# A second layer's modulation vectors: from condition matmuls in a merge stage to row products on the vector engine

## What is computed

```python
def modulation(cond, w, b):
    m = jax.nn.silu(cond) @ w + b
    return jnp.split(m, 3, axis=-1)

for l in range(DEPTH):                                   # DEPTH = 2
    sh, sc, gt = modulation(c, ada_w[l], ada_b[l])       # ada_w[l]: 1024 x 3072
    shc, scc, gtc = modulation(c_ctx, ada_w[l], ada_b[l])
    h = rms_norm(x, norm_pre[l]) * (1.0 + sc[:, None]) + sh[:, None]
    hc = rms_norm(xc, norm_pre[l]) * (1.0 + scc) + shc
    ...
    x_new = x + gt[:, None] * rms_norm(out, norm_post[l])
```

## Time and profile before

| what | value |
|---|---|
| median of 3 runs | 2044.37 us (2043.87 to 2047.22) |
| the profiled execution, its own time | 2042.73 us |
| its span, first to last instruction | 2040.9 us |
| mean granted TensorE clock | 0.986 of full |
| TensorE matmul busy | 1960.0 us, 96% |
| VectorE busy | 1296.8 us, 64% |
| ScalarE busy | 978.1 us, 48% |
| GpSimd busy | 30.3 us, 1% |
| bytes moved | 351.84 MB, mean 172 GB/s |

### The profile page before, as it was taken

The page is one execution under the profiler, slowest core; times in us unless marked ns, Lnnn a source line. Parts: engine busy times, 40 slices in busy tenths (PEclk is TensorE's granted clock), DMA queues, the critical chain, the costliest instruction groups (busy, mean ns, idle before and its releaser), DMA issues.

```text
span 2040.9 us, 29528 instructions
## 1 busy us (share of the span) xinstructions
PE 1960.0 (96%) x12558; PEld 1702.9 (83%) x12558; DVE 1296.8 (64%) x1748; ACT 978.1 (48%) x1457; POOL 30.3 (1%) x23
## 2 busy tenths in 40 slices
PE   7799999999999999999989999999999999989998
PEld 3699999899888889999878887678888888768887
DVE  3877756878645778865565565755557555676555
ACT  1355445465334546534454445554445444565444
POOL 1300000000000000000000000000000000000000
PEclk8899999999999999999999999999999999999999
DMA  7544555434676533455445554355555555525554
GB/s 307 194 155 145 163 180 170 149 125 135 212 252 229 195 128 129 144 188 181 161 140 191 186 166 161 109 167 189 189 175 178 193 186 186 176 73 176 186 187 143
DMA packets 95410, 351.84 MB, mean 172 GB/s; under 512 B 10608, under 2 KB 10736, under 8 KB 94768
## 3 DMA queue, kind: packets, MB, share of 16 engines
q1 hardware_dynamic: 94032, 341.08, 50.6%
q0 software_dynamic: 960, 7.37, 0.9%
q10 hardware_dynamic: 288, 1.51, 0.2%
HBM read 348.87 MB, written 1.05 MB: 171 GB/s over the span
## 4 chain that ended last, share of the span: by engine, by line
PE 83%; DVE 11%; ACT 3%; DMA 2%; issue 1%; SPq 0%; DVEq 0%; ACTq 0%
PE PS L551 25%; PE PS L553 24%; PE PS L552 24%; DVE w_lo L1805 3%; DMA raw<-weights 2%; ACT w_hi L1293 1%; PE PS L629 1%; PE PS L723 1%; PE PS L954 1%; PE PS L742 1%; PE PS L917 1%; PE PS L1036 1%; PE PS L806 1%; PE PS L732 0%; PE PS L1047 0%
## 5 line engine op out<-in xcount | busy, mean ns | idle before, releaser
L1805 DVE TENSOR_TENSOR w_lo<-raw,w_hi 128x1024 fp32r<-128x1024 f32 x600 | 733.2, 1232 | 400.4 <-ACT w_hi L1293 399.0
L1293 ACT ACTIVATE w_hi<-raw 128x1024 fp32r<-128x1024 f32 x600 | 624.8, 1055 | 409.4 <-DMA raw<-weights 404.7
L551 PE MATMUL PS<-h_hi,w_hi 128*128 128x256 f32 x1568 | 455.3, 290 | 14.5 <-DVE h_lo L1823 5.4
L552 PE MATMUL PS<-h_lo,w_hi 128*128 128x256 f32 x1568 | 445.2, 284 | 0.0
L553 PE MATMUL PS<-h_hi,w_lo 128*128 128x256 f32 x1568 | 445.1, 284 | 0.0
L551 PE MATMUL PS<-w_hi,h_hi 128*128 128x512 f32 (+1 forms) x1024 | 389.2, 380 | 8.7 <-DVE h_lo L2171 6.5
L553 PE MATMUL PS<-w_hi,h_lo 128*128 128x512 f32 (+1 forms) x1024 | 380.7, 372 | 0.0
L552 PE MATMUL PS<-w_lo,h_hi 128*128 128x512 f32 (+1 forms) x1024 | 379.4, 370 | 0.0
L551 PEld LDWEIGHTS PS<-h_hi,w_hi 128*128 128x128 f32 x1568 | 302.1, 193 | 33.1 <-issue 18.9
L552 PEld LDWEIGHTS PS<-h_lo,w_hi 128*128 128x128 f32 x1568 | 302.4, 193 | 0.6 <-issue 0.5
L553 PEld LDWEIGHTS PS<-h_hi,w_lo 128*128 128x128 f32 x1568 | 302.2, 193 | 0.0
(11 more groups left out here) (256 smaller groups left out, 1855.0 us busy)
## 6 DMA issues: line engine op xcount, KB each, us to landing
raw<-weights SPq DMA_DIRECT2D x642, 512.0 KB, 3.4
x<-weights SPq DMA_DIRECT2D x6, 512.0 KB, 10.2
layer<-layer_in POOLq DMA_DIRECT2D x2, 1536.0 KB, 11.4
cx<-ctx_in POOLq DMA_DIRECT2D x1, 1024.0 KB, 8.5
x<-x_in POOLq DMA_DIRECT2D x1, 1024.0 KB, 12.5
out<-arena SPq DMA_DIRECT2D x4, 256.0 KB, 2.0
consts<-consts_in POOLq DMA_DIRECT2D x1, 928.0 KB, 9.2
arena<-filter_consts_in ACTq DMA_DIRECT2D x1, 896.0 KB, 8.3
```

Of the source, the lines that this page charges most:

```text
L551: pe.matmul(dst, hi, m_hi_, start=first, stop=False, **kw)
L552: pe.matmul(dst, hi, m_lo_, start=False, stop=False, **kw)
L1293: nc.scalar.activation(w_hi[:, r, :], raw[:, r, :], ACT.Copy).then_inc(w_hi_ready, 1)
L1805: V.tensor_tensor(w_lo[:, r, :], raw[:, r, :], f32(w_hi[:, r, :]), ALU.subtract).then_inc(w_lo_ready, 1)
```

## The change

Layer 1's modulation is no longer computed with matmuls. Its weights are packed transposed: a slot now holds 128 output features by 1024 inputs, so that a feature's row lies along a partition. Both condition rows are loaded in 128 copies (`cond_in`, 1 MB), once in each of passes 0 and 1, and ScalarE takes their silu in place. For each slot VectorE makes two products, one for each condition: a scalar_tensor_tensor that multiplies slot and condition row and puts the sum along the row into one column of `ada_sums`. There are 24 slots and so 48 products, 24 in pass 0 and 24 in pass 1, three behind each attention unit's splits. The slots are loaded by GpSimd's queue into two buffers. These, the condition rows and the products' outputs lie in the area of `g_hi` and `g_lo`, which is free from the merge of one pass (or, before pass 0, from the spectra) to the gating of the next; a wait ahead of the first gate's write keeps the order. `mod_vectors(1)` reads `ada_sums`. The merge of pass 1 becomes the same as in the other passes, and the ring carries 24 slots fewer. Layer 0's modulation stays.

```diff
+ADA_ENDS = [0, 12, ADA_SLOTS]
...
-    stretch("pass1", dram_pass[0], MERGE_AT)
-    stretch("pass1_merge", None, MERGE_SLOTS + ADA_SLOTS)
-    stretch("pass1_wo", dram_pass[0] + MERGE_AT + MERGE_SLOTS, 8)
+    stretch("pass1", dram_pass[0], PASS_SLOTS)
...
+        beside = nc.alloc_sbuf_tensor_at("beside", [P, 6, SLOT], F32, offset=g_at)
+        cond_rows, ada_w, ada_prod = (beside[:, 2 * j:2 * j + 2, :] for j in range(3))
...
+        ada_sums = sb("ada_sums", [P, 48])
...
             spectrum_bias(0)
+
+            def load_ada(n):
+                pool.dma_start(ada_w[:, n % 2, :], weights[dram_pass[1] - ADA_SLOTS + n]).then_inc(ada_w_loaded[n % 2], 16)
+
+            def modulation_rows(part_):
+
+                first, end = ADA_ENDS[part_], ADA_ENDS[part_ + 1]
+                pool.wait_ge(spec_pair, DEPTH)
+                pool.dma_start(cond_rows[:, :, :], cond_in).then_inc(cond_loaded, 16)
+                load_ada(first)
+                load_ada(first + 1)
+
+                for n in range(first + 2, end):
+                    pool.wait_ge(ada_sum, 2 * (n - 1))
+                    load_ada(n)
+
+            modulation_rows(0)
+            pool.wait_ge(w_used, start["pass1"])
+            modulation_rows(1)
...
-                        if p == 1:
-                            ada(c, b, 0, i)
-                            c += 1
...
-                        if p == 1:
-                            ada(c + 1, b, 1, i)
-                            c += 1
                         pair(c + 1, 2 * b + 1)
-                    if p == 1:
-                        ada_turn(ADA_TURNS + i, 7)
...
+            def cond_silu(part_):
+
+                act.wait_ge(cond_loaded, 16 * (part_ + 1))
+                nc.scalar.activation(cond_rows[:, :, :], cond_rows[:, :, :], ACT.Silu).then_inc(cond_rows_act, 1)
...
                 splits(c0 + 6)
+                if p < 2:
+                    cond_silu(p)
                 splits(c0 + part["v"])
...
+            def ada_row(i):
+
+                n, w = divmod(i, 2)
+                dve.wait_ge(ada_w_loaded[n % 2], 16 * (n // 2 + 1))
+                if i >= 2:
+                    dve.wait_ge(ada_sum, i - 1)
+                V.scalar_tensor_tensor(ada_prod[:, w, :], ada_w[:, n % 2, :], 1.0, cond_rows[:, w, :], ALU.mult, ALU.mult,
+                                       accum_out=ada_sums[:, i:i + 1]).then_inc(ada_sum, 1)
+
+            def ada_rows_behind(p, first, end):
+                if p < 2:
+                    dve.wait_ge(cond_rows_act, p + 1)
+                    for i in range(2 * ADA_ENDS[p] + first, 2 * ADA_ENDS[p] + end):
+                        ada_row(i)
...
+                    if p < 2 and (b, j) == (0, 0):
+                        dve.wait_ge(ada_sum, 2 * ADA_ENDS[p + 1])
                     link(V.tensor_copy(g_hi[:, s, :], gd))
...
                     splits(c0 + part["v"] + 2 + 2 * n)
+                    ada_rows_behind(p, 3 * n, 3 * n + 3)
...
-                        if p == 1:
-                            ada_piece(c + 1, ADA_TURNS + i, b, (6, 7))
...
+            for c in range(0, 3 * D, P):
+                slots.append(g["ada_w"][l][:, c:c + P].T)
```

More of the change, by code:

```diff
@@ L118, in build @@
     dram = dram_pass[1] + PASS_SLOTS
-    for p in (0, 2):
+    for p in range(3):
         start[f"pass{p}_merge"] = start[f"pass{p}"] + MERGE_AT
@@ L300, in build @@
         ada_used = sem("ada_used")
+        cond_loaded = sem("cond_loaded")
+        cond_rows_act = sem("cond_rows_act")
+        ada_w_loaded = [sem(f"ada_w_loaded{j}") for j in range(2)]
+        ada_prod_ready = sem("ada_prod_ready")
+        ada_sum = sem("ada_sum")
         raw_loaded = [sem(f"raw_loaded{r}") for r in range(RING)]
@@ L413, in build @@
         block = ctx.enter_context(nc.Block())
-        def is_ada(c):
-            n = c - start["pass1_merge"]
-            return 0 <= n < MERGE_SLOTS + ADA_SLOTS and n % 5 in (0, 2)
-        def splits_to(c):
-            return c + 1 - sum(is_ada(a) for a in range(start["pass1_merge"], min(c + 1, start["pass1_wo"])))
         def f32(ap):
@@ L631, in ada_half @@
                 return mm
-            def ada(c, m, half, i):
-                if half == 0 and m == 1:
-                    pe.wait_ge(ada_taken, ADA_TURNS + i)
-                if half == 0 and m == 2:
-                    pe.wait_ge(ada_rows_ready, 3 * ADA_TURNS + 1 + 3 * i)
-                r = c % RING
-                pe.wait_ge(raw_loaded[r], 16 * (c // RING + 1))
-                ada_half(raw[:, r, :], 6 + m % 2, half).then_inc(w_used, 1)
             def ada_turn(turn, bank):
@@ L845, in run_pass @@
                 pe.wait_ge(act_evac, act_pairs(p, 9))
-                each = 5 if p == 1 else 3
                 for i in range(4):
                     for b in range(3):
-                        c = start[f"pass{p}_merge"] + each * (3 * i + b)
-                        if p == 1:
-                            ada(c, b, 0, i)
-                            c += 1
+                        c = start[f"pass{p}_merge"] + 3 * (3 * i + b)
                         pe.wait_ge(merge_free, i * 3 + (15 * p + b + 1))
@@ L1479, in run_pass @@
                 gates("gc", 2)
-                each = 5 if p == 1 else 3
                 for i in range(4):
                     for b in range(3):
-                        c = start[f"pass{p}_merge"] + each * (3 * i + b)
-                        for j in range(-1, each - 1):
+                        c = start[f"pass{p}_merge"] + 3 * (3 * i + b)
+                        for j in range(-1, 2):
                             split(c + j + AHEAD)
                         act.wait_ge(merge_free, i * 3 + (15 * p + b + 1))
-                        act.wait_ge(w_used, c + each)
+                        act.wait_ge(w_used, c + 3)
                         nc.scalar.activation(sel[:, b, :], PS[:, 2 * b + 1, :], ACT.Sigmoid).then_inc(sel_ready, 1)
@@ L2113, in run_pass @@
                 V.memset(signal[:, 1:2], 0.0).then_inc(merge_free, 1)
-                each = 5 if p == 1 else 3
                 for i in range(4):
                     for b in range(3):
-                        c = start[f"pass{p}_merge"] + each * (3 * i + b)
-                        for j in range(-1, each - 1):
+                        c = start[f"pass{p}_merge"] + 3 * (3 * i + b)
+                        for j in range(-1, 2):
                             split(c + j + AHEAD)
-                            if p == 1 and j == 2:
-                                ada_piece(c + 1, ADA_TURNS + i, b, (6, 7))
                         dve.wait_ge(sel_ready, i * 3 + (12 * p + b + 1))
@@ L2642, in pack @@
     for l in range(DEPTH):
-        token(g["ada_w"][l])
+        if l == 0:
+            token(g["ada_w"][l])
+        else:
+            for c in range(0, 3 * D, P):
+                slots.append(g["ada_w"][l][:, c:c + P].T)
         w = g["w_in"][l]
```

49 lines of the change are left out of this document (18 added, 31 removed).

## The result

The changed kernel took 2055.31 us (median of 5 runs, 2051.91 to 2058.19), the kernel before 2043.87 us (5 runs, 2042.04 to 2047.22). The ratio is 1.0054, 95% interval 1.0043 to 1.0066: **11 us slower**, 9 to 13. The profiled run of after was the median one, with a span of 2053.2 us.

What follows compares the result with a forecast made beforehand. TensorE was taken to bound the kernel (83% of the chain), with VectorE coming to bound the attention units. Pass 1 17.5 + pass 0 21.0 - merge 22.1 = +16.4 us, giving 2060 us, range 2050 to 2079 us.

Steps and rivals of the forecast that it cites:

- the likeliest case: Whole kernel: the forecast's own sum, +16.4 us to 2060 us, chance 0.80.
- What leaves: Pass 1's merge: without condition matmuls and ring slots it becomes pass 0's, 124.9 to 102.8 us, so 22.1 us go.
- What a product costs: VectorE: a 1024-element product with accumulator takes 1.28 us, of which 0.08 us for writing out the accumulator.
- The lower end: VectorE: lowest price of a product, that of a split without accumulator, 1.13 us.
- Pass 1: Attention units: products 30.7 us, less 8.8 us of VectorE waits and a 4.4 us cushion; 17.5 us reach TensorE.
- Pass 0: Attention units: 30.7 us less 7.6 us of waits and 4.1 us cushion, 19.0 us; with a late start 21.0 us.
- The cushion: End of pass 0's attention: the folded signal is ready 4.1 us before TensorE comes for it, absorbing that much lateness.
- Its start: Pass 0's first maximum: ScalarE stands for late condition rows, 0 to 4 us of lateness, taken as 2.
- At nothing: Pass 1's condition rows, second silu, weight loads, gate wait, TensorE's clock: no price; up to 3 us each for loads and clock in range.
- Rival 1: VectorE products at half throughput, two cycles an element: +51 us, 2111 us; chance 0.08.
- Rival 2: Product slots on GpSimd's queue come late, 1.1 us wait in each of 14 units: +15 us, 2075 us; chance 0.07.
- Rival 3: VectorE products in a faster mode, 0.75 us each: 25 us less than the forecast, 2035 us; chance 0.05.

Runs made afterwards that it cites:

- The counts with one and two products: Changed kernel with one or two of each three products at full width, the others 8 elements wide: 2028.20 us and 2036.65 us.
- the first pair: First profiled traces of the kernel before and the changed kernel, spans 2040.9 and 2053.2 us; up to the end of pass 2's merge the change costs 7.6 us.

## Why the prediction was right, step by step

Forecast +16.4 us and 2060, measured +11 (9 to 13) and 2055.3: the likeliest case, inside its range, with its terms too large on the side of the loss.

- **What leaves**, -22.1 us: the merge of pass 1 measured 102.9 us and -22.1. Taking the price from the same code in the other pass, instead of from a count of matmuls, was exact.
- **What a product costs**, 1.28 us: measured 1.145 us (rows 1.22 us). This is the term that was mis-sized. Two steps of it failed: the length read off the slope from 256 to 512 elements (1286 ns against 1221 measured), and the 0.08 us for the accumulator, which lies beside the next product. The lower end, "the price of a split, 1.13 us", was the truth; a split was the nearest row, the same elements on the same engine, and the forecast had it in hand. 48 x 0.135 = 6.5 us too much.
- **Pass 1**, 17.5 us: with 1.145 us the same working gives 27.5 - 8.8 - 4.4 = 14.3, measured 13.8. The 0.5 us between them are the wait as it was read: before each of six maxima 0.08 us more was free than the row in brackets says, because rows without a wait between them overlap by that much. The unit, forecast at 10.7 us, becomes 6.76 + 3.44 = 10.20, measured 10.18. The counts with one and two products follow from the same sum.
- **Pass 0**, 21.0 us: 27.5 - 7.6 - 4.1 = 15.8, measured 14.0. The cushion was as read: TensorE took the folded signal 4.1 us after it was ready in before, and waited for it in after. But VectorE had more room than the 7.6 us of waits for scores: from the first maximum to the folded signal before takes 57.6 us and after 75.5, so of 27.5 us of products 9.5 found room. The 1.9 us are the same 0.08 us ahead of seven maxima (0.6), a wait of 0.3 us for a copied slot, and 0.13 us in each of six units between the maximum and the short convolution (0.8), whose cause no row names; 0.2 us is left. Its start, taken at 2, measured 2.5, right in size by luck and wrong in cause: the condition rows landed after 5.1 us, at 99 us on the clock of the trace, and ScalarE never stood for them; the two product slots held up a ring load for 1.8 us, an overlap for which the forecast kept only a share of the range.
- **At nothing**: pass 1's condition rows and SiLU cost nothing in the first pair (flag to first maximum 170.3 us in both); the 1.5 us more in seven of eleven traces are a fall of the clock, which the forecast left to its range. The clock was 1.00 from 418 to 560 us in after, in spite of TensorE's waits; in pass 0's attention it was 0.96 where before had 1.00, and the stage still lost no more than pass 1's. The value copy's wait was overlooked, at no cost.
- **Rival 1**, half throughput: gone, 1221 ns for 1024 elements with two float32 sources from SBUF and an accumulator. A two-source subtraction of the same size takes 1222 ns. The Trainium skill, Vector Engine (DVE) Microarchitecture Reference, section Points that are easy to get wrong, has this form at half throughput; here the measurement decides against it.
- **Rival 2**, late product slots: gone, they landed after 4.5 us, the first two of pass 0, issued right behind the condition rows, after 9.1 us with 22 us to their use, and VectorE waited for none. The contention of the two engines that the Trainium skill, GPSIMD Engine Reference, section Specifications, speaks of shows in no product: only issues stood on GpSimd beside them, and a product that began at 118.93 us, with an issue at 119.31 us, was followed after 1.15 us like the others.
- **Rival 3**, a faster mode: gone, by the same row.

With 1.145 us and the measured start the forecast's own sum would have been 14.3 + 15.8 + 2.5 - 22.1 = +10.5 us, 2054 us by its base.

## What to carry to other kernels

Ask where an engine waits for another, and put added work there, in pieces no longer than the wait: the same 48 products cost 30 us behind units that had 1.2 to 1.5 us of room, and none that could be seen in the merge's steps, with 3.7 us of room in the mean. Below the room a piece is nearly free, and from there on it costs its full length. For a price take the row that has the same elements on the same engine before a slope through smaller ones. A stall that appears on an engine that doesn't pace the stage is a symptom; removing it gave nothing. Compare marks inside the traces when a difference of some 5 us matters: identical code after the last mark differed by 6 us between traces of one kernel.

## What the runs showed of the hardware

- DVE_READ_ACCUMULATOR took 84 ns in the rows and nothing in time: it starts together with VectorE's next instruction, and three products with it take 3.43 us, without it 3.41 us.
- 2 MB of loads on GpSimd's queue beside the ring's loads of 512 KB held the ring back: its loads landed after 5.4 us instead of 3.3, and ScalarE stood 7.34 us for a slot, 5.50 us with half of the 2 MB later, and at most 2.75 us with all of it elsewhere (the kernel with the products in the merge).
- Rows of 1.22 us on VectorE start 1.14 us apart when nothing is waited for. A wait in brackets is counted from the end of a row, so the room ahead of it is 0.08 us more.
- The same kernel with the same pause of TensorE (8.1 of 10 us busy) kept a granted clock of 1.00 in one trace and had 0.83 in the other, and was 1.5 us longer in that stage.
- The tail of 1050 us of unchanged code took from 1050.4 to 1057.6 us over thirteen traces (before's own two: 1052.4 and 1057.6), at mean granted clocks of 0.979 to 0.986 over the span.
